# Differential attention beside filling: one PSUM bank for a block's output, two for the filling units, and a new order of the sum of squares

## What is computed

```python
for blk in range(Sn // Q_BLOCK):                       # 4 blocks of 128 queries
    start, end = blk * Q_BLOCK, (blk + 1) * Q_BLOCK
    s = jnp.einsum('bqhme,bkhme->bhmqk', q[:, start:end], k[:, :end])
    p = jax.nn.softmax(jnp.where(allowed, s, -jnp.inf), axis=-1)
    pd = p[:, :, 0] - lam * p[:, :, 1]
    outs.append(jnp.einsum('bhqk,bkhd->bqhd', pd, v[:, :end]))
o = jnp.concatenate(outs, axis=1)
o = rms_norm(o, subln_w) * (1.0 - lam_init)            # over the 128 columns of one head
```

## Time and profile before

| | |
|---|---|
| runs of the kernel before | 1083.93, 1086.65, 1087.12 us; median 1086.65 |
| the profiled execution | 1084.3 us, its span 1082.2 us |
| busy, of the span | PE 96%, PEld 77%, DVE 57%, ACT 41%, POOL 3% |
| granted TensorE clock | 0.999 over the span |
| HBM | 133 GB/s mean |
| the steps of the attention | from about 510 to 616 us |

### The profile page before, as it was taken

How to read it: one execution, slowest core, us unless ns; L and a number is a source line. 1 busy time by engine, 2 the same in 40 slices (tenths; PEclk the granted TensorE clock), 3 DMA queues, 4 the chain that set the end, 5 groups by cost and what they waited for, 6 DMA issues and landing times.

```text
span 1082.2 us, 19329 instructions
## 1 busy us (share of the span) xinstructions
PE 1044.0 (96%) x8229; PEld 835.2 (77%) x8229; DVE 612.5 (57%) x858; ACT 449.0 (41%) x575; POOL 30.8 (3%) x50
## 2 busy tenths in 40 slices
PE   7999999999999999999989999999999999999997
PEld 5788676777776787787767778888888888878885
DVE  3489887356444479668655297762445432342346
ACT  5522742233324476756455553471222122323233
POOL 0100001000000000020000100000000000000000
PEclk9999999999999999999999999999999999999999
DMA  9978533111026321296312584304443423232202
GB/s 338 324 245 261 174 107 131 69 55 61 24 93 235 133 86 60 65 307 222 108 39 79 161 323 167 117 20 156 129 144 117 156 78 117 78 102 93 102 15 78
DMA packets 106781, 145.31 MB, mean 134 GB/s; under 512 B 3252, under 2 KB 86440, under 8 KB 106696
## 3 DMA queue, kind: packets, MB, share of 16 engines
q1 hardware_dynamic: 93544, 109.25, 30.6%
q0 software_dynamic: 5664, 21.19, 5.8%
q10 hardware_dynamic: 7488, 13.63, 3.3%
HBM read 128.33 MB, written 15.73 MB: 133 GB/s over the span
## 4 chain that ended last, share of the span: by engine, by line
PE 79%; DVE 10%; ACT 5%; DMA 2%; issue 2%; SPq 1%; ACTq 0%; POOL 0%; DVEq 0%
PE bank L2200 78%; DVE wlo L1462 2%; DVE Z L1462 1%; DMA raw<-in_w_in 1%; DVE q_lev L1462 1%; DMA qk<-early_out 1%; DVE BK L1462 1%; DVE near L1944 1%; SPq L810 1%; ACT whi L938 1%; ACT gate_row L953 1%; DVE mg L1462 1%; DVE ada_acc L1465 0%; DVE qk L1462 0%; PE bank L2783 0%
## 5 line engine op out<-in xcount | busy, mean ns | idle before, releaser
L2200 PE MATMUL bank<-hhi,whi 128*128 128x512 f32 (+1 forms) x800 | 319.7, 400 | 4.2 <-ACT gate_row L953 2.6
L2200 PE MATMUL bank<-hhi,wlo 128*128 128x512 f32 (+1 forms) x800 | 308.8, 386 | 0.0
L2200 PE MATMUL bank<-hlo,whi 128*128 128x512 f32 (+1 forms) x800 | 308.6, 386 | 0.0
L1462 DVE TENSOR_TENSOR wlo<-raw,whi 128x2048 fp32r<-128x2048 f32 (+1 forms) x80 | 166.3, 2079 | 233.7 <-ACT whi L938 227.1
L938 ACT ACTIVATE whi<-raw 128x2048 fp32r<-128x2048 f32 (+1 forms) x76 | 135.4, 1782 | 227.3 <-PE bank L2200 178.2
L2200 PEld LDWEIGHTS bank<-hhi,whi 128*128 128x128 f32 x800 | 150.2, 188 | 46.3 <-issue 10.9
L2200 PEld LDWEIGHTS bank<-hhi,wlo 128*128 128x128 f32 x800 | 150.3, 188 | 31.0
L2200 PEld LDWEIGHTS bank<-hlo,whi 128*128 128x128 f32 x800 | 150.4, 188 | 28.3 <-issue 0.7
L2200 PE MATMUL bank<-whi,d_hi 128*128 128x512 f32 x160 | 62.3, 390 | 1.2 <-DVE hid L1462 1.2
L2200 PE MATMUL bank<-whi,d_lo 128*128 128x512 f32 x160 | 62.3, 389 | 0.0
L2200 PE MATMUL bank<-wlo,d_hi 128*128 128x512 f32 x160 | 62.2, 389 | 0.0
(11 more groups left out here) (370 smaller groups left out, 1491.3 us busy)
## 6 DMA issues: line engine op xcount, KB each, us to landing
raw<-in_w_in SPq DMA_DIRECT2D x33, 1024.0 KB, 5.4
raw<-in_f_in SPq DMA_DIRECT2D x22, 1024.0 KB, 5.0
raw<-in_ada_w SPq DMA_DIRECT2D x16, 1024.0 KB, 5.0
early_out<-gate_row ACTq DMA_DIRECT2D x52, 256.0 KB, 2.4
raw<-in_f_out SPq DMA_DIRECT2D x11, 1024.0 KB, 4.8
cond<-in_ada_w SPq DMA_DIRECT2D x8, 1024.0 KB, 11.0
sg<-early_out POOLq DMA_DIRECT2D x4, 1536.0 KB, 11.7
raw<-in_w_out SPq DMA_DIRECT2D x4, 1024.0 KB, 5.0
```

The costliest lines, as they stand in the source:

```text
L1462: return v.tensor_tensor(out_, a, b, op)
L2200: return t.matmul(out_, lhsT, rhs, start=start, stop=stop, skip_group_check=True)
```

## The change

Three things. In `bank_plan` the filling units of this stretch use banks 6 and 7 by turns, and all four heads' outputs use bank 5. On TensorE the sum of squares of a step goes from the head of the step to behind its scores and its filling. On ScalarE the copy and the square of a head's output (`att`, `att2`) go ahead of the filling part of the step; Ln and Exp stay behind it.

```diff
@@ bank_plan
-                b.add("early", part[1], bank=7 if number == 2 else 6 + part[1] % 2)
+                b.add("early", part[1], bank=6 + part[1] % 2)
@@
     for h in range(4):
-        b.add("da o", h, bank=5 + h % 2)
+        b.add("da o", h, bank=5)
@@ scalar, in the loop over t_
-                if ("da", t_) in dict(EARLY[2]):
-                    early(("da", t_))
                 if h >= 0 and t_ % 4 == 1:
                     if h:
                         act.wait_ge(s_da_lo, h)
...
                     do(att2[:, :], att[:, :], ACT.Square).then_inc(s_da_sq, 1)
                     act.wait_ge(s_da_sq, up(s_da_sq))
-                elif h >= 0 and t_ % 4 == 2:
+                if ("da", t_) in dict(EARLY[2]):
+                    early(("da", t_))
+                if h >= 0 and t_ % 4 == 2:
                     act.wait_ge(*full("da ss", h))
@@ tensor, in the loop over t_
             for t_ in range(4 * TB + 3):
+                if t_ + 2 < 4 * TB:
+                    scores(t_ + 2)
+                if ("da", t_) in dict(EARLY[2]):
+                    early(("da", t_))
                 if t_ >= 6 and t_ % 4 == 2:
                     pe.wait_ge(s_da_sq, (t_ - 6) // 4 + 1)
                     ps = begin("da ss", (t_ - 6) // 4)
                     end(mm(ps[:, :], ones, att2[:, :]), "da ss", (t_ - 6) // 4)
-                if t_ + 2 < 4 * TB:
-                    scores(t_ + 2)
-                if ("da", t_) in dict(EARLY[2]):
-                    early(("da", t_))
```

## The result

Six runs of the changed kernel have a median of 1091.62 us (1090.55 to 1093.28), six of the kernel before 1086.72 us (1083.93 to 1088.05): ratio 1.0050, 95% interval 1.0039 to 1.0061. That is 4.9 us slower by the medians and 5.4 us by the ratio. The profiled execution took 1090.55 us, the fastest of the six, 6.3 us over the profiled one of before.

The account below looks back on a forecast made before the run. TensorE was taken as the bound, standing still 6.5 us in twelve places. Lost 6.08 less gained 2.57 gave net 3.5 us slower, against the median of 1086.65: 1090.1 us, range 1086.6 to 1092.4.

Parts of the forecast that it names:

- Two filling banks: Five TensorE waits for the filling unit's copy go, 2.6 us; 0.47 returns in step 8, so 2.15 us gained.
- One bank for the outputs: Next head's first product (steps 5, 9, 13, 17) needs the same step's `att` copy; covered by scores and filling, cost nothing.
- The sum's wait gone, the Ln's in its place: Steps 6, 10, 14: 0.62 us waits ahead of the sum of squares go, 0.48 us waits for Ln come; 0.42 gained.
- What is queued behind the Ln: Exponentials behind the Ln delay TensorE's scores in steps 7 and 11 by 1.91 us each; 3.12 us lost.
- Step 15: No scores left; transposes of pair 15 wait for VectorE, but two parts of filling cover it to within 0.1 us.
- The last step: Step 18: last head's chain loses its cover; TensorE starts the branch stage 4.05 us later, of which 2.96 us count.
- A pause and the clock: TensorE idle 3.9 us ahead of the branch stage; a clock fall to half would add some 0.5 us to the sum.
- a rival with a chance of 0.05: Clock rival: the branch stage starts at half clock after step 18's pause; 4.0 to 5 us slower in all, chance 0.05.

Follow-up runs that it names:

- e8: Changed kernel plus matmuls without use in both the pause of step 18 and the waits of steps 6, 7, 10, 11; 1088.38 us, ratio to before 1.0026.
- e1: Changed kernel with the sum of squares back at the head of its step, banks and ScalarE's order staying changed; 1082.77 us, ratio to before 0.9972.
- e9: Kernel of e10, but in step 18 alone the sum of squares is behind the filling; 1085.93 us, ratio to before 0.9994.
- e10: Changed kernel with the sum of squares behind the scores but ahead of the filling in every step that has one; 1082.65 us, ratio to before 0.9958.
- e6: Changed kernel plus 8 matmuls without use, into a free bank, in the pause of step 18; 1090.47 us, ratio to before 1.0044.
- e5: The changed kernel itself, run again; 1091.22 us, ratio to before 1.0053.
- e2: Kernel before with only the sum of squares moved behind the filling, banks and ScalarE's order as before; 1097.12 us, ratio to before 1.0116.
- e3: Changed kernel, but in step 18 alone the sum of squares is again ahead of the filling; 1088.89 us, ratio to before 1.0026.
- e7: Changed kernel plus matmuls without use in the waits of steps 6, 7, 10 and 11; 1089.52 us, ratio to before 1.0036.

## Why the prediction was right, and where it was short

The forecast was slower by 3.5 us against a measured 4.9, 1090.1 us against 1091.62, inside its range. The waits that it named are there, each near its size. That the total is so near is in part luck: the waits came out some 0.7 us below the sum (2.8 us by the ratio of e8, which has them without the slow clock), and the clock, which the sum put at nothing, brought 2.8 us.

- **Two filling banks** (2.15 us gained). Right in kind: no wait for `gate_row`, and step 8's 0.47 us came back as predicted (the wait for weights 0.85 instead of 0.32). In size a little low: 2.7 us in the trace of e1, and 3.0 by its ratio, interval 2.0 to 4.1.
- **One bank for the outputs** (nothing). Right: no wait for the `att` copy in any trace.
- **The sum's wait gone, the Ln's in its place** (0.62 each against 0.48). Right within 0.06: 0.48, 0.48 and 0.42 us.
- **What is queued behind the Ln** (1.91 us in steps 7 and 11). Measured 1.77 in both. Since step 7 had 0.70 before, that is 2.84 lost instead of 3.12.
- **Step 15** (within 0.1). A little low. No wait is listed, but from the product to the transposes it takes 0.89 us here where it took 0.67 before (600.33 to 601.00), and TensorE leaves the step 0.25 us later:

```profile
602.32 0.83 PE L2200 MATMUL bank<-probT,v_tok 128*128 128x128 f32 x6
603.21 0.55 PE L2783 MATMUL bank<-cst,prob 128*128 128x128 f32 x3
```

- **The last step** (TensorE 4.05 us late, of which 2.96 stay). Right in both parts, once the clock is out of the way. The wait is as summed, 3.81 us, the branch starts 4.84 us after the start of the sum against 4.95, and e9 against e10 puts TensorE 4.0 us later. That the stage behind gives back 4.05 - 2.96 = 1.09 us is seen in e6 and e8: from the start of the branch stage to the end of the second wait for `wlo` TensorE takes 17.84 us in both, against 18.91 before, 1.07 less. In the changed kernel itself both waits shrank from 2.1 to 0.2 us, because the slow clock had made TensorE the last to come.
- **A pause and the clock.** This is the term that was mis-sized: nothing in the sum, and a rival with a chance of 0.05. For the one pause that it was about, the price was fair and the chance far too low. It happened in every trace that had the pause unfilled, and cost 1.6 to 1.8 us behind the pause in four of five traces, of which the wait for `wlo` hid all but 0.4 to 0.6 (0.5 forecast); in the fifth, the changed kernel's own, it cost 2.9 and 1.7 of them stayed. What I had not considered is the second kind of place: the shorter waits of steps 6 and 7, and of 10 and 11, where 0.48 and 1.77 us stand with only the transposes between. A slow stretch there cost 1.6 us each time, with nothing behind it to hide it. e5 less e8 puts the whole share at 2.8 us.

The Trainium skill's rule ("TensorE: Matmul & The Clock Gate", section "Why this matters for your kernels"), that an idle gap between bursts lets the clock fall to half, is borne out by the traces: 0.50 for some 3 to 6 us behind the pause of 3.8 us, and 1.00 at the same place with matmuls in it (e6, e8).

The profiled executions close the sum. Measured from the first scores on (506.09 before, 506.29 after), TensorE reaches the transposes of step 6 1.6 us earlier than before, those of step 7 1.1 us later (the wait for `prob` and the slow clock), those of steps 11 and 12 2.1 us later, and the branch stage 5.4 us later. There the slow clock adds 2.9 and the waits for `wlo` give back 1.9: 6.4, with the 0.2 from ahead of the stretch 6.6, against the 6.3 us between the two spans. The medians are 4.9 apart; the profiled execution of before is one of its fastest.

Open is why the clock falls behind the same pair of waits at one place and not at another (six of ten in the traces), and why the slow stretch of the branch stage was longer in the changed kernel's own trace than in the four others.

## What to carry to other kernels

Work that fills gaps belongs behind the instruction that starts a long chain on other engines, not ahead of it: here one reordering turned the filling from a cover of Ln, Exp and the last head's chain into a delay of them. What stands in an in-order queue behind the late instruction (here the next pair's exponentials behind the Ln) is priced first; it was a wait of 1.77 us against 0.48 for the instruction itself. And a new wait of TensorE is priced with the clock behind it: waits of 0.5 and 1.8 us close together, or one of 3.8 us, cost another 1.6 to 2.9 us here, and more of it stays where no slack follows.

## What was not expected of the hardware

- Two waits of 0.48 and 1.77 us, with only the transposes between, can bring the granted clock to 0.50. The same pairs did it in one execution in step 7 alone (e2 too), in another in steps 7 and 11, and in e3 and e6 in step 11 alone.
- What a slow stretch costs is not fixed: the first 24 matmuls of the branch stage lost 2.9 us in the changed kernel's first profile, and 1.6 to 1.8 us in e2, e5, e7 and e9.
- Eight matmuls of 128x256 without use in the pause of 3.8 us kept the clock at 1.00 there.
